# Splitting a streamed weight transfer into high and low parts in one pair-wide step instead of two, inside the feed-forward loop of a decoder-layer kernel

## What is computed

```python
def rmsnorm(x, g):
    xf = x.astype(jnp.float32)
    y = xf * lax.rsqrt(jnp.mean(xf * xf, axis=-1, keepdims=True) + EPS)
    return (y * g.astype(jnp.float32)).astype(x.dtype)

        f = rmsnorm(h, g_ffn[i])
        h = h + (jax.nn.silu(f @ w_gate[i]) * (f @ w_up[i])) @ w_down[i]
        gte = jax.nn.sigmoid(rmsnorm(h, g_ple[i]) @ w_pgate[i] + b_pgate[i])
        h = h + (p[i] @ w_ple[i]) * gte
    return rmsnorm(h, g_final)
```

## Time and profile before

| | |
|---|---|
| time, median of 3 runs | 1193.62 us (1193.41 to 1194.0) |
| profiled execution | 1194.05 us, of which the traced span is 1192.0 us |
| PE busy | 1177.6 us (99% of the span) |
| DVE busy | 725.1 us (61%) |
| ACT busy | 553.6 us (46%) |
| POOL busy | 117.3 us (10%), nothing in the loop |
| TensorE clock granted | 0.996 of full speed over the span |
| DMA | 223.30 MB, mean 187 GB/s |

### The profile page before, as it was taken

How to read it: one execution, slowest core, us unless ns; L and a number is a source line. 1 busy time by engine, 2 the same in 40 slices (tenths; PEclk the granted TensorE clock), 3 DMA queues, 4 the chain that set the end, 5 groups by cost and what they waited for, 6 DMA issues and landing times.

```text
span 1192.0 us, 16308 instructions
## 1 busy us (share of the span) xinstructions
PE 1177.6 (99%) x6102; PEld 1011.1 (85%) x6102; DVE 725.1 (61%) x961; ACT 553.6 (46%) x694; POOL 117.3 (10%) x68
## 2 busy tenths in 40 slices
PE   8999999999999999999999999999999999999996
PEld 8999989988888888888888888888888888888886
DVE  4679867767665546464655555464646555467674
ACT  6453355466464444444343434434343434456553
POOL 2121444336000000000000000000000000000111
PEclk9999999999999999999999999999999999999998
DMA  9555555544657565555656556565655555555541
GB/s 331 178 177 179 183 174 173 177 165 153 209 175 252 180 208 176 196 191 183 204 177 201 186 187 199 179 205 181 191 196 180 195 188 181 206 177 176 179 174 71
DMA packets 111273, 223.30 MB, mean 187 GB/s; under 512 B 3609, under 2 KB 4449, under 8 KB 110976
## 3 DMA queue, kind: packets, MB, share of 16 engines
q1 hardware_dynamic: 111200, 222.73, 56.3%
q10 hardware_dynamic: 32, 0.01, 0.0%
HBM read 220.63 MB, written 2.10 MB: 187 GB/s over the span
## 4 chain that ended last, share of the span: by engine, by line
PE 92%; DMA 2%; DVE 2%; ACT 2%; issue 1%; POOL 1%; SPq 0%; ACTq 0%; POOLq 0%; DVEq 0%
PE ps L1008 25%; PE ps L1010 25%; PE ps L1009 25%; PE ps L1023 4%; PE ps L1024 4%; PE ps L1025 4%; DMA w_raw<-in_w_in 2%; PE ps L1033 1%; ACT w_hi L452 1%; DVE w_lo L675 0%; ACT nT_hi L473 0%; ACT junk L464 0%; PE ps L1237 0%; PE ps L1238 0%; PE ps L1274 0%
## 5 line engine op out<-in xcount | busy, mean ns | idle before, releaser
L675 DVE TENSOR_TENSOR w_lo<-w_raw,w_hi 128x1024 fp32r<-128x1024 f32 x370 | 457.1, 1236 | 436.4 <-ACT w_hi L452 435.2
L452 ACT ACTIVATE w_hi<-w_raw 128x1024 fp32r<-128x1024 f32 x408 | 432.4, 1060 | 598.0 <-PE ps L1010 493.7
L1008 PE MATMUL ps<-w_hi,nT_hi 128*128 128x512 f32 x864 | 339.0, 392 | 0.0
L1010 PE MATMUL ps<-w_hi,nT_lo 128*128 128x512 f32 x864 | 336.3, 389 | 0.0
L1009 PE MATMUL ps<-w_lo,nT_hi 128*128 128x512 f32 x864 | 336.3, 389 | 0.0
L1010 PEld LDWEIGHTS ps<-w_hi,nT_lo 128*128 128x128 f32 x864 | 162.2, 188 | 33.9
L1008 PEld LDWEIGHTS ps<-w_hi,nT_hi 128*128 128x128 f32 x864 | 162.2, 188 | 33.2
L1009 PEld LDWEIGHTS ps<-w_lo,nT_hi 128*128 128x128 f32 x864 | 162.3, 188 | 33.2
L1008 PE MATMUL ps<-w_hi,oT_hi 128*128 128x512 f32 x480 | 188.0, 392 | 0.0
L1010 PE MATMUL ps<-w_hi,oT_lo 128*128 128x512 f32 x480 | 186.9, 389 | 0.0
L1009 PE MATMUL ps<-w_lo,oT_hi 128*128 128x512 f32 x480 | 186.8, 389 | 0.0
(11 more groups left out here) (145 smaller groups left out, 556.8 us busy)
## 6 DMA issues: line engine op xcount, KB each, us to landing
w_raw<-in_w_gate SPq DMA_DIRECT2D x44, 1024.0 KB, 5.1
w_raw<-in_w_up SPq DMA_DIRECT2D x44, 1024.0 KB, 5.2
w_raw<-in_w_down SPq DMA_DIRECT2D x44, 1024.0 KB, 5.0
w_raw<-in_w_in SPq DMA_DIRECT2D x39, 1024.0 KB, 5.2
w_raw<-in_w_out SPq DMA_DIRECT2D x16, 1024.0 KB, 5.1
w_raw<-in_w_pgate SPq DMA_DIRECT2D x16, 1024.0 KB, 5.0
w_raw<-in_w_ple SPq DMA_DIRECT2D x2, 1024.0 KB, 5.5
h<-in_x SPq DMA_DIRECT2D x3, 512.0 KB, 9.9
```

Of the source, the lines that this page charges most:

```text
L452: nc.scalar.activation(slot_of(m)[0], w_raw[:, (m // 2) % RAW, rows], ACT.Copy).then_inc(hi_ready, 1)
L675: nc.vector.tensor_tensor(lo, w_raw[:, (m // 2) % RAW, rows], hi.bitcast(F32), ALU.subtract).then_inc(lo_ready, 1)
L1008: nc.tensor.matmul(banks[t][:, :], x_hi[:, k, rows], w_hi[:, s, k], start=start, stop=False)
L1010: ins = nc.tensor.matmul(banks[t][:, :], x_lo[:, k, rows], w_hi[:, s, k], start=False, stop=stop)
```

## The change

It touches the loop alone. On ACT and DVE, the two units of a transfer are split by one instruction of 128 by 2048 elements in place of two of 128 by 1024. The pair's instruction stands at the even steps, in place of the first of the two; the odd steps have none. It waits that the second of the two slots is free (`slot_free(.., m + 1, ..)`), so that a pair of slots is filled once both of their former units are done, and it counts `hi_ready` or `lo_ready` up by two at its end. DVE's waits for both high parts at once, since there is one instruction. PE's program, the transfers and what stands outside the loop are as before.

```diff
+            def split_hi_tile(m, it):
+
+                sc.wait_ge(raw_ready[(m // 2) % RAW], 16 * (m // 2 // RAW + 1) + 48 * it)
+                slot_free(sc, m + 1, it)
+                s = m % SLOTS
+                nc.scalar.activation(w_hi[:, s:s + 2].rearrange("p s k n -> p (s k) n"), w_raw[:, (m // 2) % RAW], ACT.Copy).then_inc(hi_ready, 2)
...
                         swish_of(LOOP0 + 8 + PER_LOOP * it)
-                    split_hi(LOOP0 + t + AHEAD, it)
+                    if t % 2 == 0:
+                        split_hi_tile(LOOP0 + t + AHEAD, it)
...
+            def split_lo_tile(m, it):
+
+                ve.wait_ge(hi_ready, m + 2 + PER_LOOP * it)
+                slot_free(ve, m + 1, it)
+                s = m % SLOTS
+                nc.vector.tensor_tensor(w_lo[:, s:s + 2].rearrange("p s k n -> p (s k) n"), w_raw[:, (m // 2) % RAW],
+                                        w_hi[:, s:s + 2].rearrange("p s k n -> p (s k) n").bitcast(F32), ALU.subtract).then_inc(lo_ready, 2)
...
                         add_panel(Q_DOWN + c, c, LOOP0 + t, it)
-                    split_lo(LOOP0 + t + AHEAD, it)
+                    if t % 2 == 0:
+                        split_lo_tile(LOOP0 + t + AHEAD, it)
```

## The result

The changed kernel takes 1200.12 us (median of 4, 1199.89 to 1200.91) against 1193.69 us (4 runs) for the kernel before: 6.4 us more, a ratio of 1.0053 with a 95% interval of 1.0039 to 1.0067. Slower, as forecast, inside the range, and 1.8 us beyond the 4.6 us of the sum. The profiled execution took 1199.89 us, its span 1197.9 us. The spans differ by only 5.9 us because the changed execution reached the loop 0.6 us sooner: from the first transposes of the loop to those behind it PE takes 656.42 us before (400.74 to 1057.16) and 662.90 us after (400.14 to 1063.04), 6.5 us more.

The account below looks back on a forecast made before the run. PE's products were taken to bound the loop. Ten stalls of 0.43 us plus 0.34 behind the loop gave 4.6 us more, forecast 1198.1 us, range 1194.4 to 1201.3.

Parts of the forecast that it names:

- What bounds the kernel: In the loop, PE's products set the time; savings on ACT or DVE are worth nothing, only PE waits matter.
- The long instructions: One 2048-element copy on ACT takes 1.92 us, one such subtraction on DVE 2.30 us.
- The pair's own split is hidden: At all 120 loop pairs, the split of units 20 and 21, for example, is ready 0.85 us before PE comes.
- The additions behind it are late: Panel c = 0's additions, behind the split on DVE, end at 649.36; PE needs them at 649.15: 0.21 us late.
- The size of a stall: PE ahead of unit 20: 0.21 lateness + 0.13 restart + 0.09 register instruction = 0.43 us.
- The register term: PE's wait for the additions hangs on a register instruction, adding 0.09 us, taken from DVE; possibly nothing.
- The second stall is covered by the first: Additions of c = 1, needed at unit 22, are equally late, but the 0.43 us at unit 20 covers them.
- Once more behind the loop: After the tenth iteration the transposes wait for additions: 0.21 + 0.13 = 0.34 us, the wait on the transpose itself.
- Transfers: SP gets each loop buffer 1.9 us later; 9.5 us needed of 21.7 us, so covered by 12 us.
- The gain through less disturbance of PE: Rival: fewer, longer ACT and DVE instructions shorten the loop's 2880 products; 1 ns each gives 2.9 us, 1190.7; chance 0.04.
- The long subtraction at the slow rate: Rival: DVE's long subtraction takes 2.97 us, the additions' stall 1.1 to 1.3 us, total 1206 to 1208; chance 0.05.
- Breaking up: Rival: joining costs at every pair in the loop; 0.1 us each would be 12 us, 1205.6; chance 0.02.

Follow-up runs that it names:

- the first experiment: Changed kernel with each output panel's two additions on DVE moved ahead of the pair's subtraction: 1193.73 us, ratio 1.0003.
- the eighth: Changed kernel with every panel's additions ahead of the pair's subtraction, and copy and subtraction each cut into eight instructions of 256: 1211.53 us, ratio 1.0143.
- the fifth: Changed kernel with only the additions of output panel c = 0 moved ahead of the pair's subtraction: 1199.70 us, ratio 1.005.
- the fourth experiment: Changed kernel with slots still filled in pairs, but two instructions of 1024 on each engine in place of one of 2048: 1193.85 us, ratio 1.0002.
- the seventh: Changed kernel with ACT's pair-wide copy cut into four instructions of 512, counting hi_ready only at the last one's end: 1202.78 us, ratio 1.0074.

## Why the forecast was right, point by point

- *What bounds the kernel.* Shown: DVE's busy time fell from 725.1 to 706.1 us in the changed kernel, ACT's from 553.6 to 528.6 us, and the time rose; with the additions first, the same savings give 1.0003.
- *The long instructions.* Forecast 1.92 and 2.30 us, measured 1916 and 2292 ns. The Trainium skill's 2.29 us (VectorE: DVE Perf Modes, on the errata of SBUF sources) agrees with the trace.
- *The pair's own split is hidden.* Shown by the lack of any wait of PE for `w_lo`, by the first experiment, and from the other side by the eighth. The slack is a little smaller than the 0.85 us given, by the two handoffs below: the subtraction ends at 649.51, PE's unit starts at 650.39, and with 0.13 us of restart 0.75 us is left.
- *The additions behind it are late.* This step carries the result. Shown by the first experiment (moved, the loss goes), and by the fifth (half moved, the loss stays and changes its place).
- *The size of a stall,* forecast 0.43 us, measured 0.61 by the distance of iterations. The term that was too small is the additions' lateness, 0.21 in the forecast and 0.32 in the trace: I took both handoffs, PE to ACT and ACT to DVE, from the short instructions, 0.03 and 0.04 us; here they are 0.09 us each, for the reason that the last section shows. The restart, 0.13 + 0.09 = 0.22 us in the forecast, is 0.12 us to the weight load and 0.11 more until the products are back in step (651.17 - 650.83 is 0.34, a step is 0.23), 0.23 us. The remaining 0.05 are products that follow a stall at slightly wider steps: 0.57 at the next pair, 0.02 at the one behind it, the rest further on. That part I have no cause for.
- *The register term.* The sum of the restart fits with it, 0.22 for 0.23, but its parts do not, so the fit is in part luck. From release to weight load it is 0.12 us, against 0.06 where the wait stands on the load itself (whose loads start with the transposes at 1099.29): the term is worth 0.06 and not 0.09. The loss behind it is 0.11 and not 0.07. No kernel here took the register instruction away, so that it is the cause was not tested by an edit.
- *The second stall is covered by the first.* Shown by the distance of 5.46 us and by the fifth experiment.
- *Once more behind the loop.* Forecast 0.21 + 0.06 + 0.07 = 0.34, measured 0.31 + 0.12 + 0.06 = 0.49: 0.31 us of lateness (the additions end at 1062.89), 0.12 to the weight load at 1063.01, and 0.06 more until the products are back in step. The first term is off by the same handoffs. The second was wrong in kind: the prediction has the wait on the transpose itself, and the trace has it on an instruction of its own ahead of it (line 1183, one event-semaphore instruction of 51 ns at 1062.9). In the fifth experiment it is covered, as expected: 1199.70 us there.
- *Transfers.* Forecast as hidden; no engine's wait in the loop names one.
- *The rivals.* The gain through less disturbance of PE did not come: with the additions first, where nothing else hides it, the iterations are 66.19 us apart as before. The long subtraction at the slow rate did not come: all 120 have a mean of 2292 ns. That rival also rested on a mean of unlike values. Of its four subtractions at 1486 ns on average three took 1.21 us and one 2.31 us (minimum, median, maximum):

```profile
L675 DVE TENSOR_TENSOR oT_lo<-w_raw,oT_hi x4: 1211/1213/2309, 1151.9 to 1156.4; 128x1024 fp32r<-128x1024 f32 x4
```

So there was no slower rate from which to carry on the line. The 0.24 outside the forecast's own mechanism is the sum of four rivals, where the prediction speaks of three.
- *Breaking up.* The Trainium skill's advice (Perfetto Trace Analysis, Optimizing Scalar/DVE Operations), to break up instructions where they cause bubbles though the engine isn't saturated, fits the fourth experiment against the changed kernel: the same pairs in two pieces give the 6.4 us back. But the seventh and eighth show its limit: pieces in sequence, counted only at the last one's end, lengthen the chain and cost 2.6 us more than the changed kernel and 16.6 us more than the kernel before. What helps is that the second engine may start at the first piece.

No version here is faster than the kernel before. The changed one with its additions first is level with it, with fewer instructions on two engines that have time to spare.

## What to carry to other kernels

When a step off the critical path is made longer, follow what stands behind it in its engine's order, not only the step: here the split itself kept three quarters of a microsecond of slack, and the additions queued behind it lost all of theirs. Count the slack from the event that releases the chain to the moment at which the bound engine would ask, with handoffs and restart, since here these made up more than half of the stall. Look in the trace where each wait stands: the 0.11 us that the forecast missed at each stall came from waits that had moved to instructions of their own. Work that waits for the same event as another engine's first step belongs ahead of the instruction that waits for that step.

## What was not expected of the hardware

The two handoffs, PE to ACT and ACT to DVE, are 0.09 to 0.10 us in the changed kernel and 0.03 to 0.04 us in the one before. The reason is where the wait stands. Before, the copy carries the wait that is fulfilled last, and so does the subtraction from step 4 on. In the changed kernel neither long instruction carries a wait: ahead of each stands an event-semaphore instruction, which does nothing there but wait. The views of line 263 (`slot_free`) show them, 400 to 1050 us: duration in ns (minimum/median/maximum), first and last start. Before, where ACT has none and DVE's have nothing left to wait for when they run:

```profile
L263 DVEq EVENT_SEMAPHORE  x197: 21/21/21, 410.0 to 1049.2; - x197
```

and in the changed kernel, where DVE's last until the copy is done:

```profile
L263 ACTq EVENT_SEMAPHORE  x117: 17/17/17, 400.3 to 1045.9; - x117
L263 DVEq EVENT_SEMAPHORE  x117: 21/2015/2018, 402.5 to 1045.9; - x117
```

So what is said of the change, that from step 4 on the wait for the high part stands on the split itself, does not hold for the changed kernel in the trace.

The length of the instruction is not what delays it. In the kernel with pairs of slots and short instructions the wait for the second slot stands on a register instruction ahead of the first copy, of 1024 elements. Rows of PE and ACT:

```profile
643.24 0.39 PE L1031 MATMUL ps<-w_hi,oT_lo 128*128 128x512 f32 x1
```

```profile
643.75 2.01 ACT L452 ACTIVATE w_hi<-w_raw 128x1024 fp32r<-128x1024 f32 x2 [3.43 <-PE ps L1031]
```

The product ends at 643.63, and this short copy starts 0.12 us later. Both copies start 0.045 us after the end of the instruction that waits for them, the short one here (643.703 to 643.748) and the long one of the changed kernel (645.166 to 645.211). In the copy in quarters the first piece counts nothing and carries its wait, and starts 0.04 us after PE's end (646.46 to 646.50). With the subtraction alone the short copies carry their wait and start at 0.04, and the long subtractions do not and start at 0.09 (644.68 to 644.77); with the copy alone it is the other way about (0.09 to 0.10, and 647.25 to 647.28).

What sends the wait away goes by a pattern: in all these traces an instruction that counts a semaphore up by two carries no wait, while those that count by one or not at all may carry one. No kernel here has a long instruction that counts by one, so this part was not tested by an edit.

On PE a wait on an instruction of its own costs the same: 0.12 us from release to weight load, at unit 20 (a register instruction) and behind the loop (an event-semaphore instruction), against 0.06 us with the wait on the load itself.
